# Head of a hybrid decoder layer on one Trainium2 core: idle products first, two weight pieces split by halves, x rows ahead of squares

## The reference, cut to what matters

```python
def _rmsnorm(x, g, eps=1e-6):
    xf = x.astype(F32)
    y = xf * lax.rsqrt(jnp.mean(xf * xf, axis=-1, keepdims=True) + eps)
    return (y * g.astype(F32)).astype(x.dtype)
...
    hn = _rmsnorm(x, p['norm_pre_mix'])
    z = jnp.einsum('btd,dp->btp', hn, p['w_in'])
```

## Time and profile before

| | us |
|---|---|
| median of 3 executions | 2041.51 (2041.40 to 2041.89) |
| the profiled execution | 2041.95 |
| its span, first to last instruction | 2040.2 |
| PE busy | 2022.8 (99%) |
| POOL busy | 1447.9 (71%) |
| ACT busy, DVE busy | 770.0 (38%), 705.5 (35%) |

### The profile page before, as it was taken

One profiled execution on the slowest core, in us unless ns is written; L12 is line 12 of the kernel. 1 busy time (PEld: TensorE's weight loads), 2 busy tenths in 40 slices (PEclk: granted clock), 3 DMA queues, 4 the chain that ended last, 5 costly groups with the idle time before them and its releaser, 6 DMA issues.

```text
span 2040.2 us, 39742 instructions
## 1 busy us (share of the span) xinstructions
PE 2022.8 (99%) x15890; PEld 1991.9 (98%) x15890; DVE 705.5 (35%) x1133; ACT 770.0 (38%) x950; POOL 1447.9 (71%) x1103
## 2 busy tenths in 40 slices
PE   9999999999999999999999999999999999999997
PEld 8999999999999999999999999999999999999997
DVE  5667556683533335066216311111000111111112
ACT  6365343544322234333336433333233333333331
POOL 7778755698655548788776777777777777777774
PEclk9999999999999999999999999999999999999999
DMA  7666655655544445486644454454554444444552
GB/s 260 212 183 211 204 188 186 194 170 172 153 131 132 132 158 188 146 269 228 209 146 125 153 153 145 144 154 144 152 149 150 153 147 144 154 147 145 149 151 98
DMA packets 130982, 338.22 MB, mean 166 GB/s; under 512 B 14896, under 2 KB 59036, under 8 KB 130496
## 3 DMA queue, kind: packets, MB, share of 16 engines
q1 hardware_dynamic: 113008, 315.07, 49.8%
q10 hardware_dynamic: 17872, 21.70, 3.0%
HBM read 312.84 MB, written 23.88 MB: 165 GB/s over the span
## 4 chain that ended last, share of the span: by engine, by line
PE 91%; POOL 4%; issue 2%; DVE 1%; ACT 0%; DMA 0%; SPq 0%; POOLq 0%; DVEq 0%; ACTq 0%
PE banks_g L1580 27%; PE banks_g L1582 26%; PE banks_g L1581 26%; POOL w_lo L1551 4%; PE banks_m L594 2%; PE banks_m L1717 1%; PE banks_m L1715 1%; PE banks_g L1717 1%; PE banks_g L1715 1%; PE banks_g L1716 1%; PE banks_m L1716 1%; POOL w_lo L1541 0%; PE banks_m L425 0%; DVE banks_m L2297 0%; DMA w_raw<-in_w_f 0%
## 5 line engine op out<-in xcount | busy, mean ns | idle before, releaser
L1551 POOL TENSOR_TENSOR w_lo<-w_raw,w_hi 128x512 fp32r<-128x512 f32 (+1 forms) x1088 | 1431.5, 1342 | 563.5 <-ACT w_hi L2015 238.7
L1580 PE MATMUL banks_g<-x_hi,w_hi 128*128 128x320 f32 x3168 | 987.0, 312 | 0.5 <-ACT arena L922 0.3
L1582 PE MATMUL banks_g<-x_hi,w_lo 128*128 128x320 f32 x3168 | 978.8, 309 | 0.0
L1581 PE MATMUL banks_g<-x_lo,w_hi 128*128 128x320 f32 x3168 | 978.6, 309 | 0.0
L1580 PEld LDWEIGHTS banks_g<-x_hi,w_hi 128*128 128x128 f32 x3168 | 594.6, 188 | 9.9 <-issue 5.7
L1581 PEld LDWEIGHTS banks_g<-x_lo,w_hi 128*128 128x128 f32 x3168 | 594.8, 188 | 0.2
L1582 PEld LDWEIGHTS banks_g<-x_hi,w_lo 128*128 128x128 f32 x3168 | 594.8, 188 | 0.0
L1896 ACT ACTIVATE w_hi<-w_raw 128x1024 fp32r<-128x1024 f32 (+1 forms) x256 | 266.6, 1042 | 251.7 <-PE banks_g L1582 246.9
L2015 ACT ACTIVATE w_hi<-w_raw 128x1024 fp32r<-128x1024 f32 x180 | 188.4, 1056 | 345.0 <-PE banks_g L1582 305.2
L1582 PE MATMUL banks_g<-a_hi,w_lo 128*128 128x320 f32 x704 | 217.4, 309 | 0.0
L1580 PE MATMUL banks_g<-a_hi,w_hi 128*128 128x320 f32 x704 | 217.4, 309 | 0.0
(11 more groups left out here) (388 smaller groups left out, 1742.3 us busy)
## 6 DMA issues: line engine op xcount, KB each, us to landing
w_raw<-in_w_f SPq DMA_DIRECT2D x211, 512.0 KB, 4.1
w_raw<-in_w_fi SPq DMA_DIRECT2D x176, 512.0 KB, 3.7
w_raw<-in_w_fo SPq DMA_DIRECT2D x64, 512.0 KB, 3.5
front_scratch<-ev ACTq DMA_DIRECT2D x106, 160.0 KB, 3.3
w_raw<-in_w_br SPq DMA_DIRECT2D x32, 512.0 KB, 4.9
w_raw<-in_w_o SPq DMA_DIRECT2D x32, 512.0 KB, 3.7
arena<-front_scratch SPq DMA_DIRECT2D x25, 640.0 KB, 5.6
w_raw<-in_w_fo SPq DMA_DIRECT2D x32, 384.0 KB, 3.1
```

What stands on the lines that cost most here:

```text
L1551: low = nc.gpsimd.tensor_tensor(w_lo[:, q % RING, c0:c1], w_raw[:, q % RING, c0:c1], w_hi[:, q % RING, c0:c1].bitcast(F32), ALU.subtract)
L1580: pe.matmul(out, wh, hi[:, k0 + k, :], start=first and k == 0, stop=False)
L1581: pe.matmul(out, wh, lo[:, k0 + k, :], start=False, stop=False)
L1582: mm = pe.matmul(out, wl, hi[:, k0 + k, :], start=False, stop=last and k == tiles - 1)
```

## The change

1. TensorE's idle products go to the front, ahead of its nine signals and of its waits on the banks, and a fourth of 128 columns is added.
2. SP loads `vec` before x row 0 instead of after it.
3. ScalarE makes x_hi of row 0 before the first half of piece 0's high part, and gives a signal of its own for that half (`w_hi_half`). Pieces 1 and 2 are rounded in two halves by column (rows 2p and 2p+1), with a signal behind each; TensorE waits for the half that it needs.
4. ScalarE's list is put in another order: the last x rows (10 to 15) come before most of the squares.
5. VectorE makes x_lo of rows 12 to 15 one after the other; the 13 adds of squares all follow behind them.
6. `con` is issued by ACT behind the last x rows instead of behind piece 2.

```diff
@@ tensor
+            pe.wait_ge(S("dve_order"), 1)
+            idle_products(small[:, 0:P], small[:, 0:T], M[3], 3)
+            idle_products(small[:, 0:P], small[:, 0:P], M[3], 1, P)
             nc.tensor.nop().then_inc(S("w_used"), RING)
...
             for b in range(4):
                 pe.wait_ge(S(f"evac{b}"), 1)
-            pe.wait_ge(S("dve_order"), 1)
-            idle_products(small[:, 0:P], small[:, 0:T], M[3], 3)
 
             def first_highs(p):
-                pe.wait_ge(S("w_hi_made"), p + 1)
-                for tile in first_tiles(p):
+                for n, tile in enumerate(first_tiles(p)):
+                    if n == 0 and p < 3:
+                        pe.wait_ge(S("w_hi_half"), p + 1)
+                    if n == (4 if p < 3 else 0):
+                        pe.wait_ge(S("w_hi_made"), p + 1)
                     pe.wait_ge(S("x_lo_made"), tile[0] + 1)
...
-                if row == 1:
-                    pe.wait_ge(S("w_hi_made"), 1)
+                pe.wait_ge(S("w_hi_made" if row else "w_hi_half"), 1)
@@ sync
+            sp.dma_start(vec[:, :], a["vec"]).then_inc(S("vec_in"), 16)
             sp.dma_start(xin[:, 0:1, :], a["x"][:, 0:1, :]).then_inc(S("x_first_in"), 16)
-            sp.dma_start(vec[:, :], a["vec"]).then_inc(S("vec_in"), 16)
@@ scalar
+                if p < 3:
+                    raw, hi = by_block(p)
+                    nc.scalar.activation(hi[:, :, 0:P], raw[:, :, 0:P], ACT.Copy).then_inc(S("w_hi_half"), 1)
+                    nc.scalar.activation(hi[:, :, P:2 * P], raw[:, :, P:2 * P], ACT.Copy).then_inc(S("w_hi_made"), 1)
...
-            for j in range(1, 5):
+            for j in range(1, 4):
                 first_high(j)
                 first_split(j)
-                if j == 2:
-                    act.dma_start(con[:, :], a["con"]).then_inc(S("con_in"), 16)
+            first_high(4)
+            first_high(5)
             first_square(0)
+            first_split(4)
             first_square(1)
-            first_high(5)
+            first_high(6)
+            first_high(7)
+            act.dma_start(con[:, :], a["con"]).then_inc(S("con_in"), 16)
+            first_split(5)
             first_square(2)
-            first_split(5)
+            first_split(6)
             first_square(3)
@@ vector
                 if k == 11:
                     dve.wait_ge(S("x_sq"), 1)
                     link(v.tensor_tensor(M[1][:, 0:T], xsq[:, 0, :], xsq[:, 1, :], ALU.add))
-                elif k > 11:
-                    added(2 * k - 22)
-                    added(2 * k - 21)
-            for k in range(10, KD - 1):
+            for k in range(2, KD - 1):
                 added(k)
```

More of the change, by code:

```diff
@@ L1565, in _, with idle_products @@
         def _(pe):
+            def idle_products(lhs, rhs, out, n, cols=T):
+                for _ in range(n):
+                    pe.matmul(out[:, 0:cols], lhs, rhs, start=True, stop=True)
+            pe.wait_ge(S("dve_order"), 1)
+            idle_products(small[:, 0:P], small[:, 0:T], M[3], 3)
+            idle_products(small[:, 0:P], small[:, 0:P], M[3], 1, P)
             nc.tensor.nop().then_inc(S("w_used"), RING)
@@ L1634, in first_product @@
                 return pe.matmul(G[b][:, 0:T], w[:, t * P:t * P + P], x[:, k, :], start=start, stop=stop)
-            def idle_products(lhs, rhs, out, n):
-                for _ in range(n):
-                    pe.matmul(out[:, 0:T], lhs, rhs, start=True, stop=True)
             for b in range(4):
                 pe.wait_ge(S(f"evac{b}"), 1)
-            pe.wait_ge(S("dve_order"), 1)
-            idle_products(small[:, 0:P], small[:, 0:T], M[3], 3)
             def first_highs(p):
-                pe.wait_ge(S("w_hi_made"), p + 1)
-                for tile in first_tiles(p):
+                for n, tile in enumerate(first_tiles(p)):
[3 more added lines that the diff above has]
+                        pe.wait_ge(S("w_hi_made"), p + 1)
                     pe.wait_ge(S("x_lo_made"), tile[0] + 1)
@@ L1920, in _, with by_block @@
             src, n = first_source(0)
-            first_raw, first_hi = [w[:, 0, :].rearrange("p (b n) -> p b n", b=n) for w in (w_raw, w_hi)]
+            def by_block(p):
+                return [w[:, p % RING, :].rearrange("p (b n) -> p b n", b=4) for w in (w_raw, w_hi)]
+            first_raw, first_hi = by_block(0)
             act.dma_start(first_raw[:, :, 0:P], src[:, :, 0:P]).then_inc(S("w_first_in"), 16)
@@ L1930, in first_split @@
                 act.wait_ge(S("w_used"), p + 1)
-                nc.scalar.activation(w_hi[:, p % RING, :], w_raw[:, p % RING, :], ACT.Copy).then_inc(S("w_hi_made"), 1)
+                if p < 3:
+                    raw, hi = by_block(p)
+                    nc.scalar.activation(hi[:, :, 0:P], raw[:, :, 0:P], ACT.Copy).then_inc(S("w_hi_half"), 1)
+                    nc.scalar.activation(hi[:, :, P:2 * P], raw[:, :, P:2 * P], ACT.Copy).then_inc(S("w_hi_made"), 1)
+                else:
+                    nc.scalar.activation(w_hi[:, p % RING, :], w_raw[:, p % RING, :], ACT.Copy).then_inc(S("w_hi_made"), 1)
             def first_high(j):
@@ L1939, in first_square @@
                 nc.scalar.activation(xsq[:, 2 * j:2 * j + 2, :], xin[:, 2 * j:2 * j + 2, :], ACT.Square).then_inc(S("x_sq"), 1)
-            act.wait_ge(S("w_first_in"), 16)
-            nc.scalar.activation(first_hi[:, :, 0:P], first_raw[:, :, 0:P], ACT.Copy)
             act.wait_ge(S("x_first_in"), 16)
             nc.scalar.activation(x_hi[:, 0, :], xin[:, 0, :], ACT.Copy, scale=V("g_pre", 0)).then_inc(S("x_hi_made"), 1)
+            act.wait_ge(S("w_first_in"), 16)
+            nc.scalar.activation(first_hi[:, :, 0:P], first_raw[:, :, 0:P], ACT.Copy).then_inc(S("w_hi_half"), 1)
             act.wait_ge(S("w_raw_in0"), 16)
@@ L1949, in _ @@
             nc.scalar.activation(x_hi[:, 1, :], xin[:, 1, :], ACT.Copy, scale=V("g_pre", 1)).then_inc(S("x_hi_made"), 1)
-            for j in range(1, 5):
+            for j in range(1, 4):
                 first_high(j)
                 first_split(j)
-                if j == 2:
-                    act.dma_start(con[:, :], a["con"]).then_inc(S("con_in"), 16)
+            first_high(4)
+            first_high(5)
             first_square(0)
+            first_split(4)
             first_square(1)
-            first_high(5)
+            first_high(6)
+            first_high(7)
+            act.dma_start(con[:, :], a["con"]).then_inc(S("con_in"), 16)
+            first_split(5)
             first_square(2)
-            first_split(5)
+            first_split(6)
             first_square(3)
-            first_high(6)
             first_square(4)
-            first_split(6)
-            first_high(7)
-            first_square(5)
             first_split(7)
-            first_square(6)
-            first_square(7)
+            for j in range(5, 8):
+                first_square(j)
             first_split(8)
```

## The result

The changed kernel takes 2045.64 us (median of 18 executions, 2043.46 to 2047.33); the kernel before, in the same comparison, takes 2041.49 (18 executions, 2040.94 to 2044.97). The ratio is 1.0019, with a 95% interval of 1.0012 to 1.0025: 2.4 to 5.1 us slower, at the edge of the 0.2% that can be told from no change. The predicted 2043.0 is 2.6 us too low, and the median lies 0.7 us above the range. The profiled execution took 2045.69, span 2043.9, 3.7 us more than the span before.

A forecast was written before the change was run, and what follows sets the result against it. TensorE was taken as the bound, busy 2022.8 of 2040.2 us. Start 0, half pieces 0, row 15 and the sum +1.5 all told gave 2043.45, or 2043.0 on the median; own range 2042.2 to 2043.9, full range 2040.3 to 2044.9.

The forecast's parts named there:

- Start at no cost: Head: the start was summed at 0; TensorE starts at 6.0 as now, bounds 0.5 earlier to 0.3 later.
- GpSimd with hardly a gap, one x_lo per instruction, row 15 at 30.0: Head, x rows: GpSimd's gaps close, so VectorE gets one x_lo per GpSimd instruction, 1.5 us each; row 15 at 30.0.
- Price of the first add, 0.49 or 1.5.: VectorE's first add of squares: 0.49 us with GpSimd idle, 1.5 at x_lo's pitch; row 15 at 29.0 or 30.0.
- The sum at 38.2, TensorE at 38.3.: Thirteen adds of 0.603 us and the last one follow row 15; TensorE goes on at 38.3 instead of 36.27.
- I take the middle, +1.5.: Sum of squares, +2.0 to +1.0 us over today's 36.27 all told: +1.5 was taken as the total.
- The two branches: At the sum of squares: 2.0 us lost, or 1.0 if the first add slips into GpSimd's small gap.
- the race: First add against GpSimd for the small gap ahead of piece 5, both asking within 0.1 us; called open.
- Rival B: Clock falls in the new wait at the sum: 1.5 us more, 2045.0; with a second stretch 2046.5; chance 0.08.
- Subtracting 0.44 us: The profiled execution of before lay 0.44 above the median, so 2043.45 became 2043.0 on the median.
- Cover behind the wait: Behind the sum: first mixer's loads and piece 12 come 3.5 us later, piece 12 at 40.1; covered by 4 us.
- A: Sum in time: GpSimd's gap before piece 5 stays, row 15 at about 27.0; 0.9 us won, 2040.6; chance 0.24.
- C: Nothing moves, because row 15 comes near 27.9 or the moves cancel: 2041.5; chance 0.08.

## Why the prediction was wrong, point by point

- **Start at no cost**. x_hi of row 0 was expected at 4.87 and came at 5.47 in the first profile, 4.69 in the second, both released by x's landing; the first product came at 6.77 and 5.99. So the bound "0.3 later" was too narrow: x row 0 landed 0.8 us apart in the two executions. The early clock did come (0.147 per product from the first on). Both were swallowed by the wait for row 15, as said: the lag there was -0.14 us.
- **GpSimd with hardly a gap, one x_lo per instruction, row 15 at 30.0**. Right: a gap of 0.15 us is left, as counted, and row 15 came at 29.96.
- **Price of the first add, 0.49 or 1.5.** It takes 1.59 and 1.5 of the queue, in all ten profiles in which GpSimd was inside an instruction, 0.49 in the eight in which it was idle, and 0.49 beside a busy GpSimd when an operand is in PSUM. The Trainium skill, "GPSIMD Engine Reference", section 1 (Specifications), has the contention with VectorE instructions of two SBUF inputs, and the runs agree in both directions. The trace of before already had the evidence on its side: five x_lo at 1.5, and seven adds with a PSUM operand at 0.60.
- **The sum at 38.2, TensorE at 38.3.** Right: 38.22 and 38.33, +2.06 us.
- **"I take the middle, +1.5."** First failed step, worth 0.56 us: the wait measured 2.06. The two branches were 2.0 and 1.0; the middle is a time that neither gives. Nor was the race open: GpSimd's gap was there, 0.15 us wide, and in the six profiles that have it the add began 0.11 to 0.13 us after GpSimd's next instruction and took 1.59 each time.
- **Rival B at 0.08.** The step that cost most, 1.5 us: the sum left the fall of the clock out. Its price was right to 0.1 us (1.5 us for 3.4 us at half clock), its place too, and it happened in four profiles of five. Against it I had put the 1.2-us wait at 29 us, which was followed by full pitch. That is true, but it is 1.2 and not 2.1 us, and the earlier trace rows already showed a fall behind a broken stream. With what the five profiles show, it belonged at better than even, conditional on the late sum. The Trainium skill, "TensorE: Matmul & The Clock Gate", "Why this matters for your kernels", warns of idle gaps between bursts of matmuls. The traces agree in kind, but the gap that it warns of is longer than the 2.16 us after which the clock fell here, and here the measurement decides.
- **Subtracting 0.44 us** for the profiled execution of before lying above its median. Third failed step, small: the changed kernel's first profiled execution lay at its own median (2045.69 against 2045.64), the second 0.75 below. From profile to profile the account closes: 2041.95 + 2.06 + 1.5 + 0.2 = 2045.7. For the median, 2041.49 + 3.5 = 2045.0, and the measured difference of 2.4 to 5.1 us holds it. The other 0.6 us are less than the medians here can tell, and no run places them. Rival B's own sum was 2045.0, while the range, said to reach up to it, ended at 2044.9.
- **Cover behind the wait**. Right: the loads of the first mixer came at 38.29, piece 12's at 41.06 (expected 40.1), and TensorE waited for none of them.
- **Rivals A and C.** A did not happen, but its mechanism is real: with `con` early again row 15 came at 25.98 and both waits went. C did not happen.

## What to carry to other kernels

While GpSimd subtracted from SBUF without a break, a VectorE instruction with two SBUF inputs cost a whole GpSimd instruction (1.5 us), and one with an operand in PSUM its own time (0.5 to 0.6); so put PSUM work between the slow ones, where it was free here, and do not collect it behind them. A wait of some 2 us in a full stream of products cost its length and, in four profiles of five, 1.5 us more at half the clock behind it; fill it with idle products if it can't be removed. When two branches give two times, predict one of them, and when a rival hangs on the case that you hold likeliest, give it its chance within that case.

## What the runs showed of the hardware that was not expected

- A wait of 2.1 to 2.2 us was enough for the lower clock, which then lasted 3.41 us and cost 1.5 us; with only the adds late one of two executions passed without it. The same 3.41 us at half clock near 1090 us cost nothing in the end.
- Over the 20 profiles the clock's first rise came anywhere from 4.5 to 11 us, and followed neither the idle products nor the first real product. Two executions of one kernel had it at 5.56 and 5.67, two of another at 6.17 and 8.13, two of a third at 5.72 and 8.34.
- Two adds with a PSUM operand between two x_lo cost nothing: the pitch stayed at 1.51 us for the three.
- Executions of one kernel spread by 5 to 7 us in the three kernels with `con` early, by 3 us in the two with the first square in PSUM, which have neither wait either, and by 2 us (2043.1 to 2045.0) with a late but filled one. The longest ran at a lower mean granted clock (0.996); why, and where, was not found.
